# Expert blocks in a mixture-of-experts stage: tokens gathered for two blocks at once, larger pieces of the weights

## The chip, the core and the metric

The kernel runs on one core of a Trainium2 chip. The metric is the device time in microseconds. Before the change it is 2445.29 us, the median of three runs (2442.15 to 2447.47).

## What is computed

Two transformer blocks run one after the other on 256 tokens of width 1024 in float32. The change touches only the last part of the second block, its mixture of experts: 32 experts, of which each token uses 4.

```python
logits = h @ w_router + b_router
top_val, top_idx = lax.top_k(logits, 4)
gates = softmax(top_val)
# the tokens of an expert form blocks of up to 128 rows of that expert
def expert_block(tok_b, e):
    xb = h[tok_b]
    u = xb @ w1[e] + b1[e]                       # w1[e]: 1024 x 2048
    glu = minimum(u[:, 0::2], 7.0)
    lin = clip(u[:, 1::2], -7.0, 7.0)
    act = glu * sigmoid(1.702 * glu) * (lin + 1.0)
    return act @ w2[e] + b2[e]                   # w2[e]: 1024 x 1024
out = zeros.at[slot_tok].add(slot_gate * y)      # scatter with the gates
x = layer_norm(2**0.25 * x + gt2 * out)
```

All 32 experts have to be read: 32 x (8 MB + 4 MB) = 384 MB.

## The kernel before

**Blocks.** The experts are ordered by their number of tokens. `BLOCKS` has 18 entries: `(0, 1)`, one pair, and then four times a single expert followed by three pairs. A single expert gets 128 rows of the array (`BS`), each expert of a pair 64 (`HALF`). Whatever has more tokens is done afterwards by a loop (`more`, line 2263) that the given data may skip. So four periods of four blocks follow on the first two blocks: blocks 2, 6, 10 and 14 are the single ones.

**Ring of weights.** The weights come through a ring of `MC` = 12 chunks of 1 MB (8 KB in each of 128 partitions, `chunk`, line 2078). A first matrix w1 is 8 chunks, chunk k being its rows k*128 to k*128+127, one row of 8 KB in each partition (`w1_load`, line 2083). A second matrix w2 is 4 chunks, each of two groups of 128 rows, so that a partition gets two rows of 4 KB (`w2_load`, line 2086). There are 384 chunks, numbered in the order in which TensorE uses them: w1 of block s, then w2 of block s-1. In a pair block the chunks of the two experts alternate for each k. SyncE (`moe_sync`, line 2090) issues them in that order. Before chunk n it waits (`room`, line 2093) until chunk n-12 has been used, that is until the semaphore `m_used` has reached n-12+1; the first twelve wait for the places that the stage before occupies. All these loads are issued by SyncE alone, which waits for each in turn.

**TensorE** (`moe_pe`, line 2201) does, in step s: `first(s)`, the bias and the product with w1, k outermost, 8 matmuls of 64 columns of weights x 512 for each k of a pair, 4 of 128 x 512 for a single one (line 2161, results in PSUM banks 0 to 3); `fetch(s + 1)`, two transposes of the gated selection (line 2145) and the gather of the next block's tokens as 16 matmuls of the tokens `h2` (two tiles of 128 tokens for each k) with the 0/1 selection `sel` (line 2140, banks 6 and 7); `second(s - 1)`, the product with w2 (line 2173, banks 4 and 5); eight transposes of `act` (line 2180, banks 6 and 7); and the scatter of block s-1, two halves of two matmuls (line 2185). After each chunk TensorE raises `m_used`: in a pair, both experts' chunks of one k are used in the same eight matmuls.

**ScalarE** (`moe_act`, line 2289) copies the transposed selection (line 2294) and the gathered tokens `xsT` (line 2309) out of PSUM, computes the sigmoid and copies `ys` (line 2312). **VectorE** (`moe_dve`, line 2337) computes the rest of the activation, copies `actT` (line 2354), adds the scattered results (line 2358), and builds `sel` and `selg` two blocks ahead (`select`, line 2325). The order on each engine is written out by hand, with semaphores between them. The profile shows two PE instructions for each float32 matmul of the code, and one for each transpose.

Of the kernel before, what the change touches and what calls it, by code (L numbers as in the profile page):

```python
# [220 lines left out]
def build(nc, x, out):  # L221

    with ExitStack() as ctx:
# [115 lines left out]
        xsT, actT = area(arena, [[P, KD, BS], [P, KD, BS]], 4096, 6144)  # L339
        ys, act_ = area(arena, [[P, D], [P, D]], 9216, 11264)  # L340
        sel, selg, selT = area(arena, [[P, TT, BS], [P, TT, BS], [P, 3, S]], 11264, 13312)
        rke, gwe, pcol = area(arena, [[P, TT], [P, TT], [P, 1]], 12544, 13312)
# [1740 lines left out]
        def w1_load(e, n, expert, k):  # L2083
            e.dma_start(chunk(n), x["w1_2"][0, expert, k * P:(k + 1) * P, :].rearrange("a p n -> p (a n)")).then_inc(sems(f"m_landed{n % MC}"), 16)

        def w2_load(e, n, expert, c):
            e.dma_start(chunk(n).rearrange("p (j n) -> p j n", j=2),  # L2087
                        x["w2_2"][0, expert, 2 * c * P:2 * (c + 1) * P, :].rearrange("a (j p) n -> p (a j) n", p=P)).then_inc(sems(f"m_landed{n % MC}"), 16)

        def moe_sync(e, turns):  # L2090
            expert = {0: slice(0, 1), 1: slice(1, 2)}

            def room(n):
                if n < FIRST:
                    e.wait_ge(*at("v_end", 4))
                elif n < MC:
                    e.wait_ge(*at("w_used", N_OUT2 + 3))
                else:
                    e.wait_ge(*at("m_used", n - MC + 1))

            for s in range(NBLK + 1):
                if s < NBLK:
                    blk = BLOCKS[s]
                    if s == 1:
                        e.wait_ge(*at("cnt", 1))
                    if s:
                        for r in blk:
                            expert[r] = bass.ds(e.value_load(ids[0:1, r:r + 1], min_val=0, max_val=NE - 1), 1)
                    for k in range(KD):
                        for a, r in enumerate(blk):  # L2110
                            n = W1_AT[s] + k * len(blk) + a
                            room(n)
                            w1_load(e, n, expert[r], k)
                if s:
                    blk = BLOCKS[s - 1]
                    for c in range(KD // 2):
                        for a, r in enumerate(blk):
                            n = W2_AT[s - 1] + c * len(blk) + a
                            room(n)
                            w2_load(e, n, expert[r], c)  # L2120

            def more(i, b, n):
                e.wait_ge(*at("m_used", n + MTOT))
                one = bass.ds(e.value_load(ids[0:1, bass.ds(i, 1)], min_val=0, max_val=NE - 1), 1)
                for k in range(KD):
                    w1_load(e, k, one, k)
                for c in range(KD // 2):
                    w2_load(e, KD + c, one, c)
            moe_more(e, turns, more)

        def moe_landed(pe, n):
            pe.wait_ge(*at(f"m_landed{n % MC}", 16 * (n // MC + 1)))

        def more_landed(pe, n, turn):
            pe.wait_ge(*at(f"m_landed{n}", turn * 16 + 16 * (MTOT // MC + 1)))

        def gather_pe(pe):
            for k in range(KD):
                for tt in range(TT):
                    ins = pe.matmul(banks(6, 2)[:, k * BS:(k + 1) * BS], h2[:, tt, k * P:(k + 1) * P], sel[:, tt, :], start=(tt == 0), stop=(tt == 1))  # L2140
            ins.then_inc(sems("gathered"), 1)

        def select_tp_pe(pe):
            for tt in range(TT):
                ins = pe.transpose(ps[:, 4, tt * P:(tt + 1) * P], selg[:, tt, :], ident)  # L2145
            ins.then_inc(sems("sel_tp"), 1)
# [9 lines left out]
        def up_pe(pe, w, k, at_):  # L2156

            for q in range(4):
                for a in range(w):
                    n = P // w  # L2160
                    ins = pe.matmul(ps[a * n:(a + 1) * n, q, :], xsT[:, k, a * n:(a + 1) * n], chunk(at_ + a)[:, q * 512:(q + 1) * 512],  # L2161
                                    start=False, stop=(k == KD - 1))
                    if q == 3:
                        yield ins
# [36 lines left out]
        def moe_pe(pe, turns):  # L2201

            def fetch(s):
                pe.wait_ge(*at("sel", s + 1))
                if s >= 3:
                    pe.wait_ge(*at("acc", 2 * (s - 3) + 2))
                select_tp_pe(pe)
                gather_pe(pe)

            def first(s):  # L2210
                w = len(BLOCKS[s])
                pe.wait_ge(*at("xs", s + 1))
                if s:
                    pe.wait_ge(*at("lin", s))
                else:
                    pe.wait_ge(*at("acc0", 2))
                bias_up_pe(pe, [perm[:, r:r + 1] if s else k_("own", r, 1) for r in BLOCKS[s]])
                for k in range(KD):
                    for a in range(w):
                        moe_landed(pe, W1_AT[s] + k * w + a)  # L2220
                    for ins in up_pe(pe, w, k, W1_AT[s] + k * w):
                        ins.then_inc(*up("m_used"))

            def second(s):
                w = len(BLOCKS[s])
                pe.wait_ge(*at("actT", s + 1))
                if s + 2 < NBLK:
                    pe.wait_ge(*at("selT", s + 3))
# [9 lines left out]
            fetch(0)  # L2238
            for s in range(NBLK + 1):
                if s < NBLK:  # L2240
                    first(s)
                if s + 1 < NBLK:
                    fetch(s + 1)
                if s:
                    second(s - 1)
                if s < NBLK:
                    pe.wait_ge(*at("act", s + 1))
                    if s + 1 < NBLK:
                        pe.wait_ge(*at("xs", s + 2))
                    elif s > 1:  # L2250
                        pe.wait_ge(*at("acc", 2 * (s - 2) + 2))
                    act_tp_pe(pe)
                if s:
                    pe.wait_ge(*at("ys", s))
                    scatter_pe(pe, 0, selT[:, (s - 1) % 3, :])
# [4 lines left out]
                    scatter_pe(pe, 1, selT[:, (s - 1) % 3, :])  # L2260
            pe.wait_ge(*at("acc", 2 * NBLK))

            def more(i, b, n):
                pe.wait_ge(*at("sel", n + (NBLK + 1)))
                select_tp_pe(pe)
                gather_pe(pe)
                pe.wait_ge(*at("xs", n + (NBLK + 1)))
                pe.wait_ge(*at("selT", n + (NBLK + 1)))
                bias_up_pe(pe, [pcol])
                for k in range(KD):  # L2270
                    more_landed(pe, k, n)
                    for ins in up_pe(pe, 1, k, k):
# [16 lines left out]
        def moe_act(a, turns):  # L2289
# [3 lines left out]
            def fetch(to):  # L2293
                act(selT[:, to, :], ps[:, 4, 0:S], ACT.Copy).then_inc(sems("selT"), 1)  # L2294

            a.wait_ge(*at("sel_tp", 1))
            fetch(0)
            a.wait_ge(*at("gathered", 1))
            act(xsT[:, :, :], xs_bank, ACT.Copy).then_inc(sems("xs"), 1)
            for s in range(NBLK + 1):  # L2300
                if s + 1 < NBLK:
                    a.wait_ge(*at("sel_tp", s + 2))
                    fetch((s + 1) % 3)
# [3 lines left out]
                if s + 1 < NBLK:  # L2307
                    a.wait_ge(*at("gathered", s + 2))
                    act(xsT[:, :, :], xs_bank, ACT.Copy).then_inc(sems("xs"), 1)
# [4 lines left out]
            def more(i, b, n):  # L2314
                a.wait_ge(*at("sel_tp", n + (NBLK + 1)))
                fetch(0)
                a.wait_ge(*at("gathered", n + (NBLK + 1)))
                act(xsT[:, :, :], xs_bank, ACT.Copy).then_inc(sems("xs"), 1)
# [6 lines left out]
        def select(d, s, ranks, gates_):  # L2325

            w = len(BLOCKS[s])
            n = P // w
            first = k_("slots", 0, n)
            for tt in range(TT):  # L2330
                for a, r in enumerate(BLOCKS[s]):
                    d.tensor_scalar(sel[:, tt, a * n:(a + 1) * n], first, ranks[:, tt, r:r + 1], None, ALU.is_equal)
                    ins = d.tensor_scalar(selg[:, tt, a * n:(a + 1) * n], first, ranks[:, tt, r:r + 1], gates_[:, tt, r:r + 1],
# [3 lines left out]
        def moe_dve(d, turns):  # L2337
# [23 lines left out]
            select(d, 1, rks, gws)  # L2361
            for s in range(NBLK + 1):
# [9 lines left out]
                if s + 2 < NBLK:  # L2372
                    d.wait_ge(*at("gathered", s + 2))
                    select(d, s + 2, rks, gws)
# [5 lines left out]
            def more(i, b, n):  # L2380
# [5 lines left out]
                for tt in range(TT):  # L2386
                    ts(sel[:, tt, :], at_, rke[:, tt:tt + 1], None, ALU.is_equal)
                    ins = ts(selg[:, tt, :], at_, rke[:, tt:tt + 1], gwe[:, tt:tt + 1], ALU.is_equal, ALU.mult)
# [149 lines left out]
```

## Time and profile before

| | |
|---|---|
| median of three runs | 2445.29 us |
| the profiled execution | 2449.59 us, of which its span is 2447.5 us |
| mean granted TensorE clock | 0.959 |
| TensorE matmul busy | 2228.5 us, 91% |
| VectorE / ScalarE / GpSimd busy | 750.1 / 310.8 / 102.4 us |
| stage of the experts | from 1470.8 us to the end |
| read from HBM | 575.41 MB |

The profile is that of one execution. Its page gives busy time by engine, forty slices of the span (a digit is the busy tenth of a slice), the DMA queues with packets, bytes and share of the time of 16 DMA engines, the chain of work that ended last, and groups of instructions by line. "PE" is TensorE's matmul, "PEld" its load of the stationary operand, which overlaps with matmuls; the end of a matmul is modelled, so the mean time of one is longer than the distance between two. "SPq" is SyncE's queue. Times in the views count from the start of the span.

### The profile page before, as it was taken

The numbers are of one execution on the slowest core, as the hardware profiler recorded it, in microseconds if no ns is written. First come the engines' busy times: TensorE is split into PE (matmuls) and PEld (weight loads), VectorE is DVE, ScalarE is ACT, GpSimd is POOL, SyncE is SP. The second block draws the span as 40 slices with busy tenths as digits, with TensorE's granted clock in tenths as the row PEclk, the third lists the DMA queues.
The fourth block names the chain that finished last, engine by engine and source line by source line (L and its number), as shares of the span: only waits on it lengthen the run. The fifth ranks groups of instructions, "written<-read, shape, count | busy, mean of one in ns | idle before, by whom it ended". The sixth has DMA issues, their size and how long they took to land.

```text
span 2447.5 us, 34362 instructions
## 1 busy us (share of the span) xinstructions
PE 2228.5 (91%) x15028; PEld 1376.9 (56%) x15029; DVE 750.1 (31%) x1262; ACT 310.8 (13%) x573; POOL 102.4 (4%) x117
## 2 busy tenths in 40 slices
PE   7999798999799967989898859999899999999995
PEld 5767685888477744567787543443344344334431
DVE  1000102431374325346777361212111121211123
ACT  1000101140100001243343100000000000000000
POOL 0000000000100000112212100000000000000000
PEclk9999899999899987999999959999999999999998
DMA  9545343235588930000000528999999999999995
GB/s 318 178 145 190 128 147 104 93 132 176 185 265 290 280 127 1 1 3 3 3 3 3 199 120 369 414 419 417 417 416 415 417 415 418 415 417 416 415 417 207
DMA packets 232598, 581.07 MB, mean 237 GB/s; under 512 B 10340, under 2 KB 154496, under 8 KB 199552
## 3 DMA queue, kind: packets, MB, share of 16 engines
q1 hardware_dynamic: 227472, 562.07, 60.7%
q0 software_dynamic: 4560, 14.83, 1.8%
q8 instruction: 120, 1.97, 0.3%
q10 hardware_dynamic: 416, 1.95, 0.2%
q14 instruction: 30, 0.25, 0.0%
HBM read 575.41 MB, written 3.41 MB: 236 GB/s over the span
## 4 chain that ended last, share of the span: by engine, by line
PE 81%; DVE 8%; DMA 4%; SPq 3%; ACT 2%; issue 1%; POOL 0%; DVEq 0%; ACTq 0%; POOLq 0%
PE ps L2161 18%; PE ps L467 13%; PE ps L535 10%; PE ps L2173 8%; PE ps L476 6%; PE ps L1038 4%; DMA ring<-in_w 4%; SPq L2087 3%; PE ps L2185 3%; PE ps L806 2%; PE ps L2140 2%; PE ps L627 2%; PE ps L1379 2%; PE ps L1399 1%; PE ps L1396 1%
## 5 line engine op out<-in xcount | busy, mean ns | idle before, releaser
L2161 PE MATMUL ps<-ring,arena 128*64 128x512 f32 (+1 forms) x2048 | 501.2, 593 | 13.4 <-DMA ring<-in_w 13.3
L2161 PEld LDWEIGHTS ps<-ring,arena 128*64 128x64 f32 (+1 forms) x2048 | 177.5, 143 | 335.9 <-issue 335.9
L467 PE MATMUL ps<-arena,ring 128*128 128x256 f32 x1408 | 315.4, 383 | 1.7 <-DVE arena L446 1.7
L467 PEld LDWEIGHTS ps<-arena,ring 128*128 128x128 f32 x1408 | 266.5, 191 | 49.5 <-issue 12.3
L2173 PE MATMUL ps<-ring,arena 128*64 128x512 f32 (+1 forms) x1024 | 253.8, 594 | 15.8 <-DMA ring<-in_w 15.8
L535 PE MATMUL ps<-arena,ring 128*128 128x256 f32 x1088 | 237.6, 381 | 1.4 <-DVE arena L446 0.9
L535 PEld LDWEIGHTS ps<-arena,ring 128*128 128x128 f32 x1088 | 208.0, 191 | 30.5 <-DVE arena L446 1.3
L2173 PEld LDWEIGHTS ps<-ring,arena 128*64 128x64 f32 (+1 forms) x1024 | 88.8, 143 | 168.8 <-issue 167.3
L2343 DVE TENSOR_SCALAR arena<-ps 128x1024 f32<-128x1024 f32 x18 | 22.0, 1225 | 488.1 <-PE ps L2161 488.1
L476 PE MATMUL ps<-ring,arena 128*128 128x512 f32 x352 | 157.9, 592 | 0.0
L1038 PE MATMUL ps<-arena,ring 128*128 128x256 f32 (+1 forms) x320 | 105.1, 492 | 4.6 <-DVE arena L1103 4.6
L476 PEld LDWEIGHTS ps<-ring,arena 128*128 128x128 f32 x352 | 66.9, 190 | 66.3 <-issue 64.1
L2354 DVE COPY arena<-ps 128x1024 f32<-128x1024 f32 x18 | 22.0, 1225 | 249.2 <-PE ps L2180 249.2
L1000 DVE SCALAR_TENSOR_TENSOR arena<-ring,arena 128x384 f32<-128x384 f32 x154 | 88.3, 614 | 2.5
L1038 PEld LDWEIGHTS ps<-arena,ring 128*128 128x128 f32 x320 | 61.9, 194 | 47.8 <-issue 38.3
L505 DVE TENSOR_TENSOR arena<-arena,ps 128x256 f32<-128x256 f32 x44 | 18.4, 418 | 221.9 <-ACT arena L497 221.9
L2294 ACT ACTIVATE arena<-ps 128x256 f32<-128x256 f32 x18 | 6.9, 383 | 581.5 <-PE ps L2145 581.5
L497 ACT ACTIVATE arena<-ps 128x256 f32<-128x256 f32 x44 | 16.9, 384 | 463.5 <-PE ps L467 463.5
L2185 PE MATMUL ps<-arena 128*128 128x512 f32 x144 | 66.6, 605 | 3.6 <-ACT arena L2312 2.1
L2140 PE MATMUL ps<-arena 128*128 128x128 f32 x576 | 69.2, 280 | 0.0
L2140 PEld LDWEIGHTS ps<-arena 128*128 128x128 f32 x576 | 67.8, 197 | 0.0
L2358 DVE TENSOR_TENSOR arena<-arena,ps 128x1024 f32<-128x1024 f32 x36 | 44.0, 1221 | 43.6 <-PE ps L2185 43.6
(438 smaller groups left out, 2155.0 us busy)
## 6 DMA issues: line engine op xcount, KB each, us to landing
ring<-in_w SPq DMA_DIRECT2D x384, 1024.0 KB, 17.0
ring<-in_w_in SPq DMA_DIRECT2D x26, 1536.0 KB, 6.9
ring<-in_w_ada SPq DMA_DIRECT2D x16, 1536.0 KB, 9.0
ring<-in_ffn_w_gate SPq DMA_DIRECT2D x44, 512.0 KB, 4.0
ring<-in_ffn_w_up SPq DMA_DIRECT2D x44, 512.0 KB, 5.4
ring<-in_ffn_w_down SPq DMA_DIRECT2D x44, 512.0 KB, 6.4
ring<-in_w_out SPq DMA_DIRECT2D x4, 1536.0 KB, 8.1
ring<-in_w_in SPq DMA_DIRECT2D x5, 1024.0 KB, 5.0
```

The lines of the kernel that those rows point to most:

```text
L467: ins = pe.matmul(ps[:, j % 2, half * S:(half + 1) * S], s[:, col0:col0 + P], uT[:, k, :], start=(k == 0), stop=(k == KD - 1))
L476: ins = pe.matmul(ps[:, 4 + 2 * tt + nh, :], hid[:, j % 3, tt * P:(tt + 1) * P], s[:, 2048 + nh * 512:2048 + (nh + 1) * 512], start=(j == ...
L535: ins = pe.matmul(ps[:, bank(i0 + c), 0:width], w[:, k, c * P:(c + 1) * P], src[:, k, lo:lo + width], start=(k == 0), stop=(k == kt - 1))
L627: ins = pe.matmul(ps[:, i % 4, 0:384], uT[:, k, tt * P:(tt + 1) * P], w[:, k, :], start=(k == 0), stop=(k == KD - 1))
L806: ins = pe.matmul(ps[:, 4 + 2 * tt + nh, :], src[:, k, tt * P:(tt + 1) * P], w[:, nh * 512:(nh + 1) * 512], start=(k == 0), stop=(k == KD ...
L1000: d.scalar_tensor_tensor(o, w[:, k, :], cs[:, k, m:m + 1], o, ALU.mult, ALU.add).then_inc(*up(f"ada_sum{m}"))
L1038: ins = pe.matmul(ps[:, i % 4, lo:2 * S], w[:, k, c * P:(c + 1) * P], hT2[:, k, lo:2 * S], start=(k == 0), stop=(k == KD - 1))
L2087: e.dma_start(chunk(n).rearrange("p (j n) -> p j n", j=2), x["w2_2"][0, expert, 2 * c * P:2 * (c + 1) * P, :].rearrange("a (j p) n -> p (a ...
L2140: ins = pe.matmul(banks(6, 2)[:, k * BS:(k + 1) * BS], h2[:, tt, k * P:(k + 1) * P], sel[:, tt, :], start=(tt == 0), stop=(tt == 1))
L2161: ins = pe.matmul(ps[a * n:(a + 1) * n, q, :], xsT[:, k, a * n:(a + 1) * n], chunk(at_ + a)[:, q * 512:(q + 1) * 512], start=False, stop=( ...
L2173: ins = pe.matmul(ps[a * n:(a + 1) * n, 4 + nh, :], actT[:, 2 * c + j, a * n:(a + 1) * n], chunk(at_ + a)[:, lo:lo + 512], start=(c == 0 a ...
L2185: ins = pe.matmul(ps[:, 4 + 2 * tt + nh, :], src[:, tt * P:(tt + 1) * P], ys[:, nh * 512:(nh + 1) * 512], start=True, stop=True)
```

## The change

Three things are altered, and the rest follows from them.

*Pieces of w1.* One DMA now fills two neighbouring chunks with 256 rows of w1, 2 MB. Partition p gets rows 2p and 2p+1 of these, 16 KB that lie together in memory. For a pair the order is expert a, rows of c; expert b, rows of c. Each such piece waits until both chunks that it overwrites are used.

*Pieces of w2.* They stay 1 MB, but partition p gets rows 2p and 2p+1, so 8 KB lie together. The tokens and the activation are taken apart the same way: in the gather and in the transposes of `act`, the stationary operand is every second column, starting at k % 2.

*Gather.* `fetch` handles a batch of two blocks: blocks 1 and 2, 3 and 4, and so on up to 15 and 16; block 17 is alone, as is block 0. The batch of s+1 and s+2 is gathered in step s, for even s. Its selection has 256 columns, so a matmul of the gather covers both blocks. PSUM banks 6 and 7 hold four k of both, so there are two halves: the first (8 matmuls) stands where `fetch` stood, the second (8 matmuls) in the middle of `second(s - 1)`, after ScalarE has copied the first; in step 0, which has no `second`, it follows directly. The four transposes of the selection are done together and `selT` has four places instead of three. VectorE builds both selections of a batch one after the other. `xsT` holds both blocks, and `actT` moves to free space behind the other tables.

The core of the diff (left out: the new places of the tables, the bookkeeping of semaphore counts, ScalarE's and VectorE's loops in the same pattern, and the loop `more`):

```diff
-        def w1_load(e, n, expert, k):
-            e.dma_start(chunk(n), x["w1_2"][0, expert, k * P:(k + 1) * P, :].rearrange("a p n -> p (a n)")).then_inc(...)
+        def w1_load(e, n, expert, c):
+            e.dma_start(ringf[:, (n % MC) * CHUNK:(n % MC + 2) * CHUNK].rearrange("p (j n) -> p j n", j=2),
+                        x["w1_2"][0, expert, 2 * c * P:2 * (c + 1) * P, :].rearrange("a (p j) n -> p (a j) n", j=2)).then_inc(...)

         def w2_load(e, n, expert, c):
             e.dma_start(chunk(n).rearrange("p (j n) -> p j n", j=2),
-                        x["w2_2"][0, expert, 2 * c * P:2 * (c + 1) * P, :].rearrange("a (j p) n -> p (a j) n", p=P)).then_inc(...)
+                        x["w2_2"][0, expert, 2 * c * P:2 * (c + 1) * P, :].rearrange("a (p j) n -> p (a j) n", j=2)).then_inc(...)
...
-                    e.wait_ge(*at("m_used", n - MC + 1))
+                    e.wait_ge(*at("m_used", used_at[n - MC]))
...
-                    for k in range(KD):
+                    for c in range(KD // 2):
                         for a, r in enumerate(blk):
-                            n = W1_AT[s] + k * len(blk) + a
+                            n = W1_AT[s] + 2 * (c * len(blk) + a)
                             room(n)
-                            w1_load(e, n, expert[r], k)
+                            room(n + 1)
+                            w1_load(e, n, expert[r], c)
...
-        def gather_pe(pe):
-            for k in range(KD):
+        def gather_pe(pe, n, part):
+            at_ = banks(6, 2).rearrange("p (k n) -> p k n", n=n * BS)
+            for i in range(KD // n):
+                k = part * (KD // n) + i
                 for tt in range(TT):
-                    ins = pe.matmul(banks(6, 2)[:, k * BS:(k + 1) * BS], h2[:, tt, k * P:(k + 1) * P], sel[:, tt, :], ...)
+                    ins = pe.matmul(at_[:, i, :], h2[:, tt, k // 2 * 2 * P + k % 2:(k // 2 + 1) * 2 * P:2], sel[:, tt, 0:n * BS], ...)
...
         def act_tp_pe(pe):
             for j in range(KD):
-                ins = pe.transpose(banks(6, 2)[:, j * P:(j + 1) * P], act_[:, j * P:(j + 1) * P], ident)
+                ins = pe.transpose(banks(6, 2)[:, j * P:(j + 1) * P], act_[:, j // 2 * 2 * P + j % 2:(j // 2 + 1) * 2 * P:2], ident)
...
                 for c in range(KD // 2):
+                    if c == 2 and leads(s + 2) and len(batch(s + 2)) == 2:
+                        fetch(s + 2, 1)
                     for a in range(w):
                         moe_landed(pe, W2_AT[s] + c * w + a)
...
                 if s < NBLK:
                     first(s)
-                if s + 1 < NBLK:
-                    fetch(s + 1)
+                if leads(s + 1):
+                    fetch(s + 1, 0)
+                    if s == 0:
+                        fetch(1, 1)
                 if s:
                     second(s - 1)
```

`used_at[n]` is the count of `m_used` at which chunk n has been used, which for the two chunks of a w1 piece is no longer n+1: in a pair, piece a holds the k and k+1 of one expert. `leads(s)` is true for block 0 and for odd s, `batch(s)` is the one or two blocks gathered with s.

## Rows read from the trace of the kernel before

**Rows 1.** The page: busy time, DMA slices of the span, and the issues of the stage.
```profile
PE 2228.5 (91%) x15028; PEld 1376.9 (56%) x15029; DVE 750.1 (31%) x1262; ACT 310.8 (13%) x573; POOL 102.4 (4%) x117
...
DMA  9545343235588930000000528999999999999995
GB/s 318 178 145 190 128 147 104 93 132 176 185 265 290 280 127 1 1 3 3 3 3 3 199 120 369 414 419 417 417 416 415 417 415 418 415 417 416 415 417 207
...
ring<-in_w SPq DMA_DIRECT2D x384, 1024.0 KB, 17.0
```
**Rows 2.** Windows: from:to, length, busy by engine (instructions), PEclk, DMA share, GB/s.
```profile
1500.00:1550.00 50.00, 48.22 (x264) 20.35 (x264) 10.28 (x12) 5.09 (x6) 0.00 (x0) 1.00 1.02 416
2300.00:2350.00 50.00, 49.88 (x254) 19.53 (x252) 8.47 (x7) 3.49 (x4) 0.00 (x0) 1.00 1.02 414
```
**Rows 3.** Waits of the expert stage, 1440 to 2447: us in total, times, longest.
```profile
PE ps L2173 <- DMA ring<-in_w: 15.8, 13, 1.5
...
PE ps L2161 <- DMA ring<-in_w: 13.3, 10, 2.5
```
**Rows 4.** Chain of waits, 1400 to 2447: start us, us, engine and line.
```profile
1498.46 0.37 PE ps L2145 x2
1498.83 3.59 PE ps L2140 x32
1502.44 1.03 ACT arena L2309
1503.61 1.06 PE ps L2180 x8
...
1548.30 3.68 PE ps L2173 x16
...
1585.73 3.57 PE ps L2140 x32
...
1609.08 27.62 PE ps L2161 x128
...
1760.55 3.68 PE ps L2173 x16
...
2184.86 3.68 PE ps L2173 x16
...
2417.38 3.67 PE ps L2173 x16
```
**Rows 5.** DMA queues at 1500 to 1512, 1993 to 2011 and 11 to 18: packets, MB, share.
```profile
q1 hardware_dynamic: 697, 5.06, 101.3%
...
q1 hardware_dynamic: 1865, 7.37, 102.3%
...
q10 hardware_dynamic: 139, 1.84, 62.5%
```
**Rows 6.** Line 2084, the one issue at 1474.5, at 1509.5, 1612.8 and 1664.0.
```profile
DMA to landing us min/median/max: 4.8/4.8/4.8
...
DMA to landing us min/median/max: 10.8/10.8/10.8
...
DMA to landing us min/median/max: 8.1/8.1/8.1
...
DMA to landing us min/median/max: 7.1/7.1/7.1
```
**Rows 7.** The page: groups of lines 467 and 2140, busy us, mean ns of one.
```profile
L467 PE MATMUL ps<-arena,ring 128*128 128x256 f32 x1408 | 315.4, 383 | 1.7 <-DVE arena L446 1.7
...
L2140 PE MATMUL ps<-arena 128*128 128x128 f32 x576 | 69.2, 280 | 0.0
L2140 PEld LDWEIGHTS ps<-arena 128*128 128x128 f32 x576 | 67.8, 197 | 0.0
```

More of the change, by code:

```diff
@@ L2124, in more @@
                 one = bass.ds(e.value_load(ids[0:1, bass.ds(i, 1)], min_val=0, max_val=NE - 1), 1)
-                for k in range(KD):
-                    w1_load(e, k, one, k)
+                for c in range(KD // 2):
+                    w1_load(e, 2 * c, one, c)
                 for c in range(KD // 2):
@@ L2131, in moe_landed, with batch, leads, place @@
         def moe_landed(pe, n):
[L2132 removed]
+            piece, count = landed_n[n]
+            pe.wait_ge(*at(f"m_landed{piece}", count))
         def more_landed(pe, n, turn):
[L2135 to L2138 removed]
+            pe.wait_ge(*at(f"m_landed{n}", turn * 16 + (starts[n] + 16)))
+        def batch(s):
+            return [s] if s == 0 else [b for b in (s, s + 1) if b < NBLK]
+        def leads(s):
+            return s < NBLK and (s == 0 or s % 2 == 1)
+        def place(s):
+            return 0 if s % 2 else int(s > 0)
+        def gather_pe(pe, n, part):
+            at_ = banks(6, 2).rearrange("p (k n) -> p k n", n=n * BS)
+            for i in range(KD // n):
+                k = part * (KD // n) + i
                 for tt in range(TT):
[L2140 removed]
+                    ins = pe.matmul(at_[:, i, :], h2[:, tt, k // 2 * 2 * P + k % 2:(k // 2 + 1) * 2 * P:2], sel[:, tt, 0:n * BS], start=(tt == 0), stop=(tt == 1))
             ins.then_inc(sems("gathered"), 1)
[L2143 to L2145 removed]
+        def select_tp_pe(pe, n):
+            for a in range(n):
+                for tt in range(TT):
+                    ins = pe.transpose(ps[:, 4, a * S + tt * P:a * S + (tt + 1) * P], selg[:, tt, a * BS:(a + 1) * BS], ident)
             ins.then_inc(sems("sel_tp"), 1)
@@ L2218, in first @@
                 for k in range(KD):
-                    for a in range(w):
-                        moe_landed(pe, W1_AT[s] + k * w + a)
-                    for ins in up_pe(pe, w, k, W1_AT[s] + k * w):
+                    if k % 2 == 0:
+                        for a in range(w):
+                            moe_landed(pe, w1_at(s, k, a))
+                    for ins in up_pe(pe, w, k, lambda a: w1_at(s, k, a), place(s) * BS):
                         ins.then_inc(*up("m_used"))
@@ L2291, in moe_act, with turned_in, gathered_in @@
             xs_bank = banks(6, 2).rearrange("p (k n) -> p k n", k=KD)
[L2293 to L2299, printed above, removed]
+            copied = [0, 0, 0]
+            def turned_in(s):
+                copied[0] += 1
+                a.wait_ge(*at("sel_tp", copied[0]))
+                for i, b in enumerate(batch(s)):
+                    act(selT[:, b % 4, :], ps[:, 4, i * S:(i + 1) * S], ACT.Copy).then_inc(sems("selT"), 1)
+            def gathered_in(s, part):
+                copied[1] += 1
+                n = len(batch(s))
+                a.wait_ge(*at("gathered", copied[1]))
+                act(xsT[:, part * (KD // n):(part + 1) * (KD // n), 0:n * BS], banks(6, 2).rearrange("p (k n) -> p k n", n=n * BS), ACT.Copy).then_inc(sems("xs"), 1)
+            turned_in(0)
+            gathered_in(0, 0)
             for s in range(NBLK + 1):
-                if s + 1 < NBLK:
-                    a.wait_ge(*at("sel_tp", s + 2))
-                    fetch((s + 1) % 3)
+                if leads(s + 1):
+                    turned_in(s + 1)
                 if s < NBLK:
@@ L2306, in moe_act @@
                     act(sig, glu, ACT.Sigmoid, scale=1.702).then_inc(sems("sig"), 1)
-                if s + 1 < NBLK:
-                    a.wait_ge(*at("gathered", s + 2))
-                    act(xsT[:, :, :], xs_bank, ACT.Copy).then_inc(sems("xs"), 1)
+                if leads(s + 1):
+                    for part in range(len(batch(s + 1))):
+                        gathered_in(s + 1, part)
                 if s:
@@ L2314, in more @@
             def more(i, b, n):
[L2315 to L2318, printed above, removed]
+                a.wait_ge(*at("sel_tp", n + (copied[0] + 1)))
+                act(selT[:, 0, :], ps[:, 4, 0:S], ACT.Copy).then_inc(sems("selT"), 1)
+                a.wait_ge(*at("gathered", n + (copied[1] + 1)))
+                act(xsT[:, :, 0:BS], xs_bank, ACT.Copy).then_inc(sems("xs"), 1)
                 a.wait_ge(*at("glu", n + (NBLK + 1)))
@@ L2371, in moe_dve @@
                         add(tt, 2 * (s - 1) + tt + 1)
-                if s + 2 < NBLK:
-                    d.wait_ge(*at("gathered", s + 2))
-                    select(d, s + 2, rks, gws)
+                if leads(s + 1):
+                    read[0] += len(batch(s + 1))
+                if leads(s + 3):
+                    d.wait_ge(*at("gathered", read[0]))
+                    for b in batch(s + 3):
+                        select(d, b, rks, gws)
             d.wait_ge(*at("acc", 2 * NBLK))
```

95 lines of the change are left out of this document (64 added, 31 removed).

## The prediction

> **What bounds the kernel now.** I read the page first. TensorE is busy for nine tenths of the span, but from slice 25 on the DMA engines stand at 9 and near 416 GB/s too [rows 1], so in the expert stage, the last 977 us, two engines claim to be full. The windows of that stage confirm it: of 17 windows of 50 us between 1500 and 2350 the first and the last have TensorE busy 48.22 and 49.88 us, the clock granted in full, beside a DMA share of 1.02 at 416 and 414 GB/s; the 15 between show 1.01 or 1.02 [rows 2]. Which of the two is the bound shows in the list of waits: in the whole stage TensorE waits 13.3 + 15.8 = 29.1 us for pieces of the ring [rows 3], and the DMA engines do not pause. The chain of waits shows the rhythm: TensorE starts the last quarter of a second matrix right after a landing at 1548.3, at 1760.55 and, two periods on, at 2184.86 [rows 4]. A period (one single block, three pair blocks; 84 pieces of 1 MB, 56 of first matrices and 28 of second ones) takes (2184.86 - 1760.55) / 2 = 212.15 us. The stage is bound by the DMA stream, and TensorE is only some 6 us in a period (29.1 over 4.5 periods) faster than it.
>
> Check of that by rates. A first-matrix piece has 8 KB runs: 5.06 MB in 12 us [rows 5], so 1.0486 MB take 2.49 us. A second-matrix piece has 4 KB runs: 7.37 MB in 18 us [rows 5], so 2.56 us. 56 x 2.49 + 28 x 2.56 = 211.1 us; the remaining 1.0 us of a period is loss that I leave as it is.
>
> **How much the queue holds.** A piece issued into an empty queue lands after 4.8 us, of which 2.49 are its data; so 2.3 us pass from issue to the first byte that counts. Pieces issued at 1509.5, 1612.8 and 1664.0 land after 10.8, 8.1 and 7.1 us [rows 6]. Less 4.8, the queue there still had 6.0, 3.3 and 2.3 us of work. Those are the thin places: TensorE has just done work that frees no ring space (gather, transposes, scatter). If the issue at such a place comes later than this, the DMA engines stand still, and as they are the bound, that time is never made up.
>
> **The change, part by part.**
>
> (a) *Second matrices, 8 KB runs.* 128 pieces go from 2.56 to 2.49 us, which is what the same geometry costs now in the first matrices: -0.07 each, -9.0 us of stream in all. I take this as certain.
>
> (b) *First matrices, 16 KB runs.* No row has 16 KB runs. The nearest is the constants' load with runs of 14,396 bytes: 1.84 MB in 62.5% of 7 us is 420.6 GB/s of occupied time; the 8 KB row gives by the same sum 5.06 MB / (1.013 x 12 us) = 416.3 [rows 5]. The ratio is 1.010, so 2.49 becomes about 2.46 us: -0.03 for each of 244 pieces after the first twelve, -7.3 us. Bounds: 2.44 (twice that advantage) and 2.56 (the 4 KB row, should the doubled spacing of addresses hurt as much as halved runs do).
>
> (c) *Pieces of 2 MB: release.* This is the term that the change doesn't show. TensorE uses the ring in the order k, expert. Before, a piece is one k of one expert and is free after that k. Now a piece is k and k+1 of one expert, so both pieces of a pair block come free only after the second k. A k step of a pair is 27.62 / 8 = 3.45 us [rows 4]. So wherever a first-matrix piece overwrites first-matrix pieces of a pair, its first half is issued 3.45 us later. SP waits twice and everything behind it in SP's queue waits too, all of it loads of the same stream. Once at the start this simply shifts the stream: the first piece beyond the ring is issued at 1474.5 + 3.45 (queue empty, all twelve pieces landed long before): +3.45 us.
>
> (d) *Gather of two blocks at once.* I count as the profile does, two float32 matmuls for each in the code. Before, every block has 2 transposes (0.37 us) and 32 matmuls over 128 columns (3.57 us) [rows 4], 3.94 together. Now every second block has 4 transposes (0.74) and 2 x 16 matmuls over 256 columns (4 k x 2 token tiles x 2 in each half). The nearest row with 256 columns and 128x128 weights is line 467: 1408 in 315.4 us, 0.224 each [rows 7]; I take 0.22, 16 make 3.5 us. Sum 7.75 against 2 x 3.94 = 7.88: TensorE gains 0.1 us in two blocks, nothing. Bounds: 16 x 0.112 = 1.8 us a half if the columns came free (the spacing of the 128-column ones), 16 x 0.38 = 6.1 if they did not overlap at all (the mean of one in the row). But the work moves: all 7.75 us now stand in the step of the single block (and two steps on), where 3.94 stood: +3.8 us before the next block starts.
>
> (e) *Strided weights.* Gather and the transposes of act now read every second float as the stationary operand. No row before has a strided stationary operand. The weight loads of the gather take 0.197 us and its matmuls are 3.57 / 32 = 0.112 us apart [rows 4, 7], so a load is longer than its slot already and still hidden. I value it at nothing; the upper bound is a load at half the rate: hidden under 0.22 us in the gather, but 8 x 0.11 = 0.9 us more in the eight transposes (1.06 us now [rows 4]) of each block. Below nothing there is no room, since the same floats are read. The Trainium skill (SBUF — State Buffer, "Door 1: The DMA port swizzle") says that reads that hit a 16-byte line at least twice run at full rate, which a step of two floats does; by it the sum stays as it is, without it, it is the third rival's. No run so far shows it.
>
> (f) *ACT and DVE.* Copies of the gathered tokens stay two of 1.03 us per two blocks, selections the same number; both engines idle for most of each 51 us block. Only at the very start is there no second matmul to hide the half-way copy: gather, copy, gather, copy before act is turned is 0.74 + 3.5 + 1.05 + 3.5 + 1.05 = 9.8 us for 5.0 now, +4.8 on TensorE. With 3.45 of (c) the issue at 1509.5 comes 8.3 us later; the queue had 6.0 and its stream is 3.45 - 16 x 0.03 = 3.0 late: 9.0 covers 8.3, just. Cost nothing; if that cover were gone, a microsecond.
>
> **The thin place of each period.** It is the issue at 1612.8, freed by the first k of the pair block after the single one. From the landing at 1548.2, where TensorE and stream meet, TensorE comes there 3.8 (d) + 3.45 (c) = 7.25 us later. The stream has moved 28 pieces in that time (8 first ones of the single block, 8 second ones, 12 first ones of the pair block) and is 20 x 0.03 + 8 x 0.07 = 1.2 us earlier. It had 3.3 in hand: 7.25 + 1.2 - 3.3 = 5.15 us in which the DMA engines are empty, in each period. The next thin place (1664.0) has its gather already behind it: TensorE comes 3.45 - 0.1 = 3.3 late, the stream 5.15 - 1.2 - (16 x 0.03 + 4 x 0.07) = 3.2, and 2.3 are in hand; it holds. So a period costs -56 x 0.03 - 28 x 0.07 + 5.15 = +1.5 us, 213.7 instead of 212.15. TensorE's own work, some 206 us, stays below it. What the faster runs give, the empty queue takes back and a little more.
>
> **Sum.** Four such places: 4 x 1.5 = +6.0. Pieces outside these four periods (372 - 336 = 36; 20 first, 16 second): -1.7. Start: +3.45. The end is as before: the last pieces are still 1 MB, TensorE's 3.67 us after the last landing at 2417.4 and the tail follow [rows 4]. Together +7.8 us. The profiled execution takes 2449.6 with its surroundings (span 2447.5) and would become 2457.4; the median of the runs shown is 4.3 lower, so the median becomes 2445.3 + 7.8 = 2453.1 us.
>
> **Rivals.**
> - *Each piece has a fixed cost, and half as many save half of it.* If the 2.3 us from issue to first byte were paid by every piece, 122 fewer would take 281 us off: 2164 us. The rows exclude it: pieces land 2.49 us apart, less than 4.8, so the 2.3 us are paid only where the queue is empty, and there I count them. Chance 0.00. The Trainium skill (DMA: Bandwidth & Descriptors, "Anatomy of one DMA") has such a fixed cost, about 2.0 us, and would have transfers as large as can be; as an estimate from it, 244 us.
> - *The queue never runs dry* (SP's release is early enough, or the gather half is much shorter than 3.5 us). Then the rates count in full: 3.45 - 7.3 - 9.0 = -12.9, 2432 us. For it: the median issue lands after 17.0 us [rows 1], so mostly the queue is deep. Against: 8.1 us at 1612.8. It decides from 7.25 us of delay falling under 2.1 (3.3 less 1.2). Chance 0.12.
> - *It balances*: the dry time is some 3.5 us in a period, because a half gather takes nearer 2.7 us or 16 KB runs reach 2.44; then -2 to +4, around 2446. Chance 0.13.
> - *Strided weights cost double loads*: two sets of transposes lie between the meeting point and the thin place, 1.8 us more dry time, four times: +7, 2460 us. For it: no row shows such an operand. Against: loads are hidden today beyond their slot. Chance 0.11.
> - *16 KB runs bring nothing or hurt*: at 2.49 a period has 36 pieces that pay and 20 that only shorten the dry time: 0.03 x (244 - 80) = +4.9, 2458; at the 4 KB rate +16, 2469. Chance 0.14.
> - The forecast as summed, from 2449 to 2456: chance 0.50.
>
> **How the numbers follow.** No change is what lies within 0.2%, 4.9 us, of 2445.3, about what a measurement of this kernel can tell. Faster: 0.12 of the first rival and 0.02 of the second: 0.14. Same: the rest of the second and the low end of the forecast, 0.11 + 0.07 = 0.18. Slower: 0.43 + 0.11 + 0.14 = 0.68. The range 2441 to 2464 leaves out the first rival (0.12) and the worse half of the last one (0.05).
>
> **What would show it.** The DMA share should no longer be 1.02 throughout but have a hole of about 5 us once a period, right at the first two k of the block behind each single one. The stream of second matrices should move at 421 GB/s, that of first ones at 422 to 430. An issue after that hole lands after 4.8 + 2.5 us. TensorE's waits for the ring should rise from 29 to some 37 us, although TensorE does the same work. The forecast is wrong if there is no hole, if 16 matmuls over 256 columns take well under 3.5 us, or if the eight transposes of act take more than 1.1 us.

## The result and the profile after

The changed kernel takes 2453.22 us in the median of 12 runs (2448.50 to 2459.11), the kernel before beside it 2443.63 us (12 runs). The ratio is 1.0033, 95% interval [1.0023, 1.0044]: slower by 0.33%, or 8.1 us; the medians are 9.6 us apart. The profiled execution took 2453.23 us, with a span of 2451.4 us. Its span is only 3.9 us longer than the one before, because the part ahead of the experts, whose code is the same, was 5.4 us shorter in that execution (its first expert matmul starts at 1465.5, not at 1470.8). So stages are compared: 2451.4 - 1465.5 = 985.9 us now, 2447.5 - 1470.8 = 976.7 us before, +9.2 us.

From the page of the changed kernel, the DMA slices and the two kinds of issue. In place of the even 414 to 419 GB/s [rows 1] there is 425 with a dip to 378 to 386 once in every period:

```profile
DMA  9555442335588930000000629999999999999995
GB/s 319 176 155 180 137 153 88 103 128 185 178 272 284 283 111 1 1 3 3 3 3 3 228 90 397 425 386 425 425 378 426 425 425 380 426 424 380 426 425 219
...
ring<-in_w SPq DMA_DIRECT2D x128, 2048.0 KB, 16.6
ring<-in_w SPq DMA_DIRECT2D x128, 1024.0 KB, 17.4
```

The chain of waits of the changed kernel, in the expert stage: start, us, what. First step 0 (two halves of the gather with a copy behind each), then the step of the first single block, the pair block behind it, and the starts of a last quarter of a second matrix a period apart:

```profile
1493.09 0.59 PE ps L2177 x4
1493.68 3.47 PE ps L2171 x16
1497.17 1.03 ACT arena L2361
1498.25 3.74 PE ps L2171 x16
1502.02 1.03 ACT arena L2361
1503.19 1.19 PE ps L2215 x8
...
1582.57 0.44 PE ps L2177 x4
1583.01 3.46 PE ps L2171 x16
1586.47 7.02 PE ps L2208 x32
1593.49 3.66 PE ps L2171 x16
...
1610.06 27.62 PE ps L2196 x128
...
1759.37 3.65 PE ps L2208 x16
...
2187.57 3.65 PE ps L2208 x16
...
2421.25 3.68 PE ps L2208 x16
```

A period is (2187.57 - 1759.37) / 2 = 214.1 us, for 212.15 before [rows 4].

Windows of the changed kernel (PE, PEld, DVE, ACT, POOL busy, then the granted clock, DMA share, GB/s) ahead of, in and behind the hole, and one of 3 us somewhat later:

```profile
1605.00:1612.00 7.00, 7.00 (x37) 2.57 (x38) 5.33 (x12) 0.26 (x1) 0.00 (x0) 1.00 1.00 428
1612.00:1620.00 8.00, 8.00 (x40) 2.68 (x38) 0.79 (x4) 0.00 (x0) 0.00 (x0) 1.00 0.37 119
1620.00:1627.00 7.00, 7.00 (x36) 2.35 (x34) 0.00 (x0) 0.00 (x0) 0.00 (x0) 1.00 1.00 426
1681.00:1684.00 3.00, 3.00 (x10) 1.20 (x8) 0.00 (x0) 0.00 (x0) 0.00 (x0) 0.52 1.01 421
```

The middle row is the hole: a share of 0.37 in 8 us leaves 5.0 us of the DMA engines' time unused, while TensorE is busy throughout; for 3.5 us of it, from 1614.7 on, no engine has a packet. Before, every window had 1.01 or 1.02 [rows 2]. The share counts the time in which packets are under way, and that is not the whole loss: the 119 GB/s of the same row, beside 428 and 426 ahead and behind, are 8 x (1 - 119 / 427) = 5.8 us of the stream. The packets at the edges of the hole take longer for their bytes (322 GB/s to a full share, for 427). So both losses are given below, by the share and by GB/s.

DMA queues of the changed kernel at 1714 to 1729 (first matrices) and 1998 to 2010 (second ones):

```profile
q1 hardware_dynamic: 444, 6.46, 101.1%
...
q1 hardware_dynamic: 693, 5.06, 101.3%
```

6.46 MB in 15 us is 431 GB/s, so 2.43 us a chunk (2.49 before); 5.06 MB in 12 us is 422, 2.49 us (2.56 before) [rows 5]. And the landings of the 2 MB pieces issued at 1472.6 (empty queue), 1512.6, 1617.3 and 1664.7, which answer to [rows 6]:

```profile
DMA to landing us min/median/max: 7.6/7.6/7.6
...
DMA to landing us min/median/max: 7.8/7.8/7.8
...
DMA to landing us min/median/max: 7.7/7.7/7.7
...
DMA to landing us min/median/max: 10.6/10.6/10.6
```

TensorE's waits for the ring in the whole stage (total, times, longest), 33.3 us for 29.1 before [rows 3]:

```profile
PE ps L2196 <- DMA ring<-in_w: 22.6, 11, 2.7
...
PE ps L2208 <- DMA ring<-in_w: 10.7, 10, 1.3
```

### The profile page after: what moved, and what is told of

Its sections match the earlier page's. It is cut to its first block, busy times and chain, and to the rows that moved or that the text cites. A ratio compares the mean times of both kernels' runs of the same rounds, so it can differ in the third digit from the quotient of the medians.

```text
span 2451.4 us, 33546 instructions
## 1 busy us (share of the span) xinstructions
PE 2229.1 (91%) x14772; PEld 1371.5 (56%) x14773; DVE 748.7 (31%) x1262; ACT 309.7 (13%) x573; POOL 102.2 (4%) x117
## 3 DMA queue, kind: packets, MB, share of 16 engines
q10 hardware_dynamic: 416, 1.95, 0.2%
## 4 chain that ended last, share of the span: by engine, by line
PE 80%; DMA 9%; DVE 8%; ACT 2%; issue 1%; SPq 0%; POOL 0%; DVEq 0%; ACTq 0%; POOLq 0%
PE ps L2196 16%; PE ps L467 13%; PE ps L535 10%; DMA ring<-in_w 8%; PE ps L2208 8%; PE ps L476 6%; PE ps L1038 4%; PE ps L2171 3%; PE ps L2220 2%; PE ps L806 2%; PE ps L627 2%; PE ps L1379 2%; PE ps L1399 1%; PE ps L1396 1%; PE ps L1409 1%
## 5 line engine op out<-in xcount | busy, mean ns | idle before, releaser
L497 ACT ACTIVATE arena<-ps 128x256 f32<-128x256 f32 x44 | 16.9, 384 | 461.4 <-PE ps L467 461.4
L2171 PE MATMUL ps<-arena 128*128 128x256 f32 (+1 forms) x320 | 68.9, 372 | 1.1 <-ACT arena L2361 1.1
L2171 PEld LDWEIGHTS ps<-arena 128*128 128x128 f32 x320 | 59.0, 206 | 11.6 <-issue 5.7
L2370 ACT ACTIVATE arena<-arena 128x1024 f32<-128x1024 f32 x18 | 19.0, 1057 | 319.7 <-DVE arena L2407 319.7
```

The source lines that it names most:

```text
L2171: ins = pe.matmul(at_[:, i, :], h2[:, tt, k // 2 * 2 * P + k % 2:(k // 2 + 1) * 2 * P:2], sel[:, tt, 0:n * BS], start=(tt == 0), stop=(tt ...
```

## The experiments

The ratio is against the kernel before, timed beside each kernel. "Us" of a ratio is its part of 2445; an interval is some 2 to 4 us to either side. A stage is the span less the start of the first expert matmul, in one profiled execution: 976.7 us before, 985.9 us changed.

**halves_held** - the 2 MB piece as two DMAs, the wait for both chunks kept.

```diff
                             room(n)
                             room(n + 1)
-                            w1_load(e, n, expert[r], c)
+                            w1_half(e, n, expert[r], c, 0)      # rows 0::2 of 256, 8 KB runs
+                            w1_half(e, n + 1, expert[r], c, 1)  # rows 1::2
```

> The changed kernel, but each 2 MB piece of a first matrix is loaded as two 1 MB DMAs (8 KB runs, every second row), both issued only when both of its chunks are free, as now; each chunk has its own landing. Theory A (late release and the moved gather let the queue run dry): the hole at the block behind each single one stays, about 4.5 us a period (0.7 less than in the changed kernel because the stream in front of it is slower), and since the first matrices go back from 2.445 to 2.485 us a chunk, the time is about 11 us over the kernel before, 6 over the changed one. Theory B (the size of one DMA and of what TensorE has to wait for is what costs): the holes go, time 5 us under the kernel before.

2458.18 us, ratio 1.0055 [1.0041, 1.0069], +13 us. Two windows of it, ahead of and in the hole:

```profile
1600.00:1610.00 10.00, 10.00 (x54) 3.92 (x52) 4.01 (x6) 1.02 (x1) 0.00 (x0) 1.00 1.01 421
1610.00:1620.00 10.00, 10.00 (x48) 3.29 (x46) 2.12 (x11) 0.00 (x0) 0.00 (x0) 1.00 0.50 179
```

The hole of 5 us (share 0.50 of 10; 5.7 us by 179 GB/s in place of 421) is there with 1 MB DMAs and 8 KB runs. So the size of one DMA does not make it. Theory B is out as the cause of the hole.

**halves** - the same DMAs, each issued when its own chunk is free. With that the order of the four DMAs of a pair changes too, from a, a, b, b to a, b, a, b; "late release" below means both, and no run parts them.

```diff
+                        for j in range(2):
                             for a, r in enumerate(blk):
-                                n = W1_AT[s] + 2 * (c * len(blk) + a)
+                                n = W1_AT[s] + 2 * (c * len(blk) + a) + j
                                 room(n)
-                                room(n + 1)
-                                w1_half(e, n, expert[r], c, 0)
-                                w1_half(e, n + 1, expert[r], c, 1)
+                                w1_half(e, n, expert[r], c, j)
```

> As halves_held, but each 1 MB half is issued as soon as its own chunk is free, in the order of use, so the late release is gone and the gather of two blocks stays. Theory A: hole of about 1 us a period, first matrices at 2.485 us; about 5 us under the kernel before, 16 under halves_held. Theory B: same time as halves_held. Theory C (the strided stationary operand costs): both stay over the kernel before.

2448.30 us, ratio 1.0010 [1.0001, 1.0019], +2 us. Early release takes 11 us off halves_held (10 by the medians); A had 16, and 5 us under the kernel before, which was missed by 7. The windows show where most of the 7 us are, not what is behind them:

```profile
1600.00:1610.00 10.00, 10.00 (x54) 3.94 (x52) 3.83 (x5) 1.02 (x1) 0.00 (x0) 1.00 0.96 373
1610.00:1620.00 10.00, 10.00 (x50) 3.41 (x48) 2.30 (x12) 0.00 (x0) 0.00 (x0) 1.00 0.93 370
```

There is no hole, yet the share is 0.96 and then 0.93 where a full queue has 1.01: 1.3 us lost in 20. By the share that is hardly more than the hole of 1 us that A had already counted. By GB/s it is 20 x (1 - 371.5 / 422) = 2.4 us in a period, 1.4 us more than A had, so some 5.6 us in four periods, of the 7 missed. The queue loses time already when it is nearly empty. I took it for full or empty.

**gather_two** - the kernel before with the gather of the change alone. This kernel and w2_runs are the changed one with the rest turned back, so their tables lie where the change puts them; the diffs show them against the kernel before, in short.

```diff
-                    fetch(s + 1)                       # in every step, 16 matmuls over 128 columns
+                    fetch(s + 1, 0)                    # s even: 8 over 256 columns,
+                    ...                                # 8 more in the middle of second(s - 1)
```

> The kernel before with only the gather of two blocks at once: loads, runs, release and contiguous stationary operands as before. Theory A: the moved 3.8 us use up the 3.3 us in hand at the thin place, hole of about 0.4 us a period, +1.6 us in all (within noise of the kernel before). A rival in which the gather alone empties the queue: 5 us a period, +20 us.

2450.54 us, ratio 1.0023 [1.0014, 1.0032], +6 us; +1.6 was expected. Again the thin place, and again more lost than the 0.4 us of full and empty (share 0.90 in 10 us, 1.1 us; by 343 GB/s in place of 423 it is 1.9 us):

```profile
1600.00:1610.00 10.00, 9.88 (x44) 3.78 (x40) 2.44 (x2) 1.02 (x1) 0.00 (x0) 1.00 1.02 423
1610.00:1620.00 10.00, 10.00 (x59) 3.31 (x60) 3.67 (x13) 0.00 (x0) 0.00 (x0) 1.00 0.90 343
```

**w2_runs** - the kernel before with 8 KB runs in the second matrices.

```diff
-                        x["w2_2"][0, expert, 2 * c * P:2 * (c + 1) * P, :].rearrange("a (j p) n -> p (a j) n", p=P)
+                        x["w2_2"][0, expert, 2 * c * P:2 * (c + 1) * P, :].rearrange("a (p j) n -> p (a j) n", j=2)
...
-                ins = pe.transpose(..., act_[:, j * P:(j + 1) * P], ident)
+                ins = pe.transpose(..., act_[:, j // 2 * 2 * P + j % 2:(j // 2 + 1) * 2 * P:2], ident)
```

> The kernel before with only the second matrices in 8 KB runs (and act turned with strided stationary operand). Theory A: 128 chunks go from 2.56 to 2.485 us, no hole, -9.6 us. Theory C (strided operand costs 0.9 us a block on TensorE): TensorE gains 16 us of work against 27 us of waits, -3 us or less.

2437.03 us, ratio 0.9968 [0.9956, 0.9979], -8 us. Step (a) of the prediction stands by itself, with its strided transposes: theory C had 3 us or less here, which the interval (5 to 11 us faster) leaves out.

**halves_one** - halves with the gather of one block in each step.

```diff
         def batch(s):
-            return [s] if s == 0 else [b for b in (s, s + 1) if b < NBLK]
+            return [s]
         def leads(s):
-            return s < NBLK and (s == 0 or s % 2 == 1)
+            return s < NBLK
```

> As halves (two 1 MB DMAs of 8 KB runs for each piece of a first matrix, each issued in the order of use as soon as its own chunk is free), but the gather is one block in each step, as before the change. First of a square of four with halves, halves_held and held_one: gather of one or two blocks, release early or late. Theory A: neither delay is left, the queue never runs dry, second matrices at 2.485 us: 9 us under the kernel before, like w2_runs. Theory C (strided stationary operands in gather and transposes cost): clearly slower than w2_runs.

2437.59 us, ratio 0.9965 [0.9952, 0.9978], -9 us. Level with w2_runs, though the gather too now has strided stationary operands. With w2_runs, which tests the transposes, this puts theory C out.

**held_one** - halves_held with that same edit.

> As halves_held (late release), but the gather is one block in each step. Theory A: the 3.45 us of late release alone meet 3.3 us in hand less what the faster second matrices take from it; holes of some 1.5 us behind the single block and again one block later, +3 to +8 us over the kernel before, 6 or more under halves_held (2458). Rival D (only the moved gather matters): -9 us, like halves_one.

2453.09 us, ratio 1.0024 [1.0013, 1.0035], +6 us. Windows at the two thin places:

```profile
1610.00:1620.00 10.00, 10.00 (x48) 3.30 (x46) 0.00 (x0) 0.00 (x0) 0.00 (x0) 1.00 0.85 331
1660.00:1670.00 10.00, 10.00 (x48) 3.29 (x46) 0.00 (x0) 0.00 (x0) 0.00 (x0) 1.00 0.91 355
```

Shares of 0.85 and 0.91 instead of 1.01 are 1.6 and 1.0 us, one block apart, as A said. By 331 and 355 GB/s in place of 422 they are 2.2 and 1.6 us, 3.7 in this period. The square of four, in us of the ratio:

| | release early | release late |
|---|---|---|
| gather of one block | -8.6 (halves_one) | +5.9 (held_one) |
| gather of two blocks | +2.4 (halves) | +13.4 (halves_held) |

Late release costs 14.5 and 11.0 us, the moved gather 11.0 and 7.5 us. Together they cost 22.0, and each by itself on top of halves_one adds up to 25.5; a difference of 3.5 is within the intervals.

**pieces_one** - the changed kernel (16 KB runs) with the gather of one block, by the same edit.

> The changed kernel (2 MB pieces with 16 KB runs, second matrices in 8 KB runs) with the gather of one block in each step. Theory A: stream 11 us faster than in held_one at most, but then it comes sooner to the thin places, which return most: holes of 3 and 2 us in a period, +4 to +8 us over the kernel before, so within a few us of the changed kernel. Rival E (the gather of two blocks is what made the change slow): 15 us or more under the changed kernel, 2438.

2457.35 us, ratio 1.0053 [1.0040, 1.0067], +13 us; +4 to +8 was expected, so this was missed by 5 or more. Rival E, 15 us under the changed kernel, is out. With the long runs the gather of two blocks is even 4 to 5 us better than that of one (4.9 by the ratios, whose intervals just touch, 4.1 by the medians, 990.1 and 985.9 us by the stages). The windows show three thin places in a period instead of one:

```profile
1590.00:1600.00 10.00, 10.00 (x48) 3.30 (x46) 0.00 (x0) 0.00 (x0) 0.00 (x0) 1.00 0.83 323
...
1610.00:1620.00 10.00, 10.00 (x50) 3.37 (x48) 0.00 (x0) 0.00 (x0) 0.00 (x0) 1.00 0.73 275
1660.00:1670.00 10.00, 10.00 (x50) 3.43 (x48) 0.98 (x5) 0.00 (x0) 0.00 (x0) 1.00 0.86 329
```

With the 1.01 of a full queue they lose 1.8, 2.8 and 1.5 us: 6.1, more than the one hole of 5.0 in the changed kernel. By GB/s, with 428 for full, it is 2.5, 3.6 and 2.3 us, over 8, for 5.8. It is 7 us worse than held_one, although its runs are longer. Two things differ: the stream is faster and so comes sooner to the thin places, and a piece lands, and restarts the queue, only as a whole. No run parts these two, and how much each does is open.

**mixed** - the candidate: gather of one block (edit as in halves_one, not shown), 16 KB runs for the first six k, halves for the last two. Against halves_one only `apart` differs.

```diff
+        def apart(s, c):
+            return c == 3
...
                     for c in range(KD // 2):
+                        for j in range(2 if apart(s, c) else 0):
+                            for a, r in enumerate(blk):
+                                n = W1_AT[s] + 2 * (c * len(blk) + a) + j
+                                room(n)
+                                w1_half(e, n, expert[r], c, j)
-                        for a, r in enumerate(blk):
+                        for a, r in enumerate([] if apart(s, c) else blk):
```

> The candidate for a better version: gather of one block, second matrices in 8 KB runs, first matrices in 2 MB pieces with 16 KB runs for the first six k, but the last two k (the pieces at the thin places, and the first piece beyond the ring) as 1 MB halves issued as soon as their own chunk is free. Theory A: 192 of 256 first chunks at 2.445 us, no hole or one of 1 us: 11 to 16 us under the kernel before, below w2_runs. If late release costs at other places too: no better than w2_runs.

2433.08 us, ratio 0.9958 [0.9943, 0.9972], -10 us by the ratio, -13 by the medians. Faster than both kernels. 11 to 16 us and "below w2_runs" were expected, and that it is below is not shown: the intervals of w2_runs, halves_one and mixed overlap widely. The stages of w2_runs and halves_one are 967.7 and 967.4 us, that of mixed is 965.4, and its median is 4.5 us below that of halves_one. That hints at 2 to 4 us from 192 chunks with 16 KB runs, where the rates alone (0.05 us a chunk) would give 10. Its windows at both thin places and over a longer stretch with both kinds of matrices:

```profile
1600.00:1620.00 20.00, 20.00 (x105) 6.61 (x106) 2.77 (x9) 0.00 (x0) 0.00 (x0) 1.00 1.00 416
1650.00:1670.00 20.00, 20.00 (x102) 6.56 (x102) 3.92 (x10) 0.00 (x0) 0.00 (x0) 1.00 0.98 403
1800.00:1850.00 50.00, 50.00 (x235) 20.76 (x232) 10.03 (x15) 3.49 (x4) 0.00 (x0) 1.00 1.01 423
```

And its waits for the ring, 15.9 us for 29.1 before:

```profile
PE ps L2223 <- DMA ring<-in_w: 8.4, 7, 1.4
PE ps L2211 <- DMA ring<-in_w: 7.5, 4, 2.5
```

**mixed_two** - mixed with the gather of two blocks.

> mixed, but with the gather of two blocks at once as in the change. Whether that gather gains anything once the release is early. Theory A: TensorE's work is the same, but the moved 3.8 us open a hole of 2 to 3 us a period again: 4 to 8 us under the kernel before, 7 over mixed. Rival F (fewer matmuls for the gather are a gain once the late release is away): mixed or faster.

2443.15 us, ratio 0.9977 [0.9966, 0.9989], -6 us: 5 us worse than mixed by the ratios (10 by the medians, 6 by the stages, 971.3 and 965.4 us). Where the release is early, the gather of two blocks costs again, through the queue:

```profile
1600.00:1610.00 10.00, 10.00 (x46) 4.10 (x43) 1.41 (x2) 1.64 (x2) 0.00 (x0) 1.00 0.97 397
1610.00:1620.00 10.00, 10.00 (x56) 3.23 (x56) 4.71 (x14) 0.00 (x0) 0.00 (x0) 1.00 0.81 324
```

Shares of 0.97 and 0.81 in place of 1.01: 2.4 us lost in a period, and 3.0 us by GB/s.

**mixed_wide** - mixed with `return c == 3 or (s > 2 and s % 4 in (0, 3))`.

> mixed, but in the two pair blocks behind each single one all pieces of the first matrices are 1 MB halves, so that the queue holds a little more at both thin places and 96 of 256 chunks instead of 192 keep 16 KB runs. Theory A with a reserve that counts before the queue is quite empty (as the run halves suggests, 8 us slower than its hole of 1 us allows): 11 to 13 us under the kernel before, level with mixed. If only run length counts: 4 us over mixed.

2434.61 us, ratio 0.9955 [0.9943, 0.9968], -11 us. Level with mixed: half the number of 16 KB chunks, no loss that can be seen. That the reserve at the thin places makes up for the shorter runs fits this, but is not shown, since 96 long runs more or less are worth no more than the noise.

## Why the prediction was right

The forecast was 2453.1 us; the median is 2453.22. That the two are 0.1 us apart is luck: the forecast stood on a median of 2445.29 us, and beside the changed kernel the one before took 2443.63. What can be compared is the difference: +7.8 us forecast, +8.1 by the ratio, +9.6 by the medians, +9.2 by the stages. By its own steps:

- *The DMA stream is the bound.* Right. w2_runs shortens the stream alone and the time follows by 8 us, for 9.0 in step (a).
- *(b), 16 KB runs.* 2.46 us a chunk was taken, 2.43 measured. From 422 to 431 GB/s a chunk gains 0.05 us, where the 14,396 byte row gave 0.03.
- *(c), late release.* Right as a mechanism: at equal DMAs it costs 11 to 14.5 us. At the start the first issue beyond the ring came 1472.6 - 1465.5 = 7.1 us after the first matmul, for 1474.5 - 1470.8 = 3.7 before: +3.4, as said.
- *(d), the gather.* 0.44 + 3.46 + 3.66 = 7.6 us for two blocks, 7.75 forecast. The halves came as valued, 3.5 us each; the four transposes took 0.44 us in these steps and 0.59 in others, not 0.74.
- *(e), strided operand.* The eight transposes take 1.16 to 1.19 us, 0.1 more than before, where I had nothing and 0.9 as the end. More than 1.1 us was one of my signs that the forecast is wrong. This sign came, and it was set too tight: 0.1 us a block is far from the 0.9 of the rival. The view of line 2215 of the changed kernel (min/median/max ns of a load of the transposes) has

```profile
L2215 PEld LDWEIGHTS ps<-const,arena x144: 194/209/219, 1503.2 to 2405.7; 128*128 128x128 f32 x144
```

  where the same loads took 140 in the median before. In w2_runs they take 209 ns too, and it gains 8 us all the same; TensorE is not the bound. The Trainium skill (SBUF — State Buffer, "Door 1: The DMA port swizzle") has reads that hit a 16-byte line at least twice at full rate, as a step of two floats does. For these loads the trace does not agree, 209 against 140 ns, while those of the gather went only from 192 to 197.
- *(f), step 0.* From the end of `first(0)` to the transposes 1503.19 - 1493.09 = 10.1 us, 5.15 before; the issue at 1512.6 lands after 7.8 us, which is what an empty queue gives a 2 MB piece (7.6). The 0.7 us in hand were used up, and from 1510 to 1520 the stream moved 388 GB/s (422 before), 0.8 us that were put at nothing.
- *The thin place.* 5.15 us of standstill in a period were forecast, at the block behind the single one. It is there, with 5.0 us by the share and 5.8 by GB/s; the period became 214.1, for 213.7 forecast. At 1664.7 the piece lands after 10.6 us, so that place holds.
- *Two misses that cancel.* At the measured rates the data of a period take 56 x 0.05 + 28 x 0.08 = 5.0 us less, where the forecast had 3.6. The period is 1.95 us longer all the same, so the stream loses about 7.0 us more in it than before, where the forecast had 5.15. The standstill was undervalued by 1.8 us and the gain of the runs by 1.4; that the sum came out is in part luck.
- *Sum.* 4 x 1.95 for the periods and +3.4 at the start are 11.2 us; the stage has +9.2, so -2.0 are left for the rest (-1.7 forecast). 7.8 was forecast in all.
- *Waits.* 33.3 us, 37 forecast.

One thing was right in the sum and wrong in its parts. The hole was counted as 3.8 (gather) + 3.45 (release) + 1.2 - 3.3, which reads as if without the moved gather it would shrink to 1.35 us. pieces_one shows that it does not: the loss splits over three thin places and grows, to 6 us by the share and 8 by GB/s. The late release alone is enough for a slower kernel. And the steps counted a queue as full or empty; gather_two and halves missed by 4 and 7 us because a nearly empty one already loses.

The rivals: *never dry* is refuted by the hole, *strided weights cost loads* by the transposes, which took 0.1 us more and not 0.9, together with w2_runs and halves_one, *16 KB runs hurt* by the rate of 431 GB/s, *it balances* by the ratio's interval, which begins at 1.0023, or 5.6 us. That fewer DMAs save a fixed cost each found no support: halves_held, with twice as many DMAs for the first matrices, differs from the changed kernel by 5 us, about the 6 that its slower runs were expected to cost. Pieces that queue up do not pay the 2.3 us of an empty queue one by one: they move at 2.43 and 2.49 us a chunk. The Trainium skill (DMA: Bandwidth & Descriptors, "Anatomy of one DMA") gives its 2.0 us for DMAs that GpSimd issues, while these are SyncE's.

## What to carry to other kernels

When the stream that fills a ring bounds the kernel, what a larger piece costs is the later release: a piece can be issued only when its last part is free. Look for the issues with the shortest time to landing; what is above that of an empty queue is the reserve, and whatever delays issues or speeds the stream up is paid from it. Measure a loss of the stream by GB/s and not by the share of busy time alone: in halves the share showed 1.3 us of 2.4. Long runs move the stream faster where the queue is deep, and both kinds of piece can stand in one stream; but of the 10 us that they promised in mixed, only 2 to 4 are seen, not clear of the noise, and small pieces without the late release (halves_one) already take 9 us off the kernel before.

## What the runs showed of the hardware

A nearly empty queue loses time before it stands still: in halves the share is 0.96 and 0.93 and the rate 373 and 370 GB/s, for 421 in a full window, with no gap as such. The cause was not tested.

TensorE's granted clock fell to 1.2 GHz inside the stage of the changed kernel: 0.52 in the window 1681 to 1684 above, right behind a wait of 2.1 us for the piece of 1665.25, which ended at 1680.35 in the chain of waits. It fell three times; the waits ahead of the other two were 2.4 and 2.7 us. In the kernel before the stage ran at 1.00 up to its tail, though it too had a wait of 2.5 us, so the length of a wait alone does not tell. One fall cost 1.7 us of TensorE's time: the 32 instructions of line 2196 behind the wait took 8.78 us, and 32 of them at the full clock, from 1657.46 on, 7.07. No loss of the DMA stream shows behind it (421 GB/s in that window).

Packets of 16 KB move at 431 GB/s, of 8 KB at 422 and of 4 KB at 410 [rows 5]: doubling the run gave 12 GB/s, and doubling it again 9.
